# Expert stage of a one-core trunk kernel: gathered rows turned by VectorE instead of TensorE, low parts shared with GpSimd

## The chip, the cores and the metric

The kernel runs on one core of one Trainium2 chip, as one program. The metric is the device time of an execution in microseconds. Each of the core's engines (TensorE, VectorE, ScalarE, GpSimd and SyncE) runs its own instruction stream, and the streams meet only in semaphores.

## The reference, cut to what matters

The reference is one layer of a decoder trunk: three gated token mixers, an output projection, a layer norm, a mixture of experts with a router, and a second layer norm. The change touches the experts only. Each of 1024 tokens goes to two of 32 experts:

```python
def expert_block(args):
    xblk, e = args                                   # 128 gathered rows of 1024 features
    h = jax.nn.silu(xblk @ w_gate[e]) * (xblk @ w_up[e])   # 1024 x 512 each
    return h @ w_down[e]                             # 512 x 1024
y = jnp.zeros((N, D)).at[tok_sorted].add(yb[dest] * gate_sorted[:, None])
```

All of it is float32, and the kernel keeps that accuracy by splitting each operand in two.

## The kernel before

The stage `experts` handles one block of 128 slots for each of the 32 experts; an expert with more tokens than that is finished in a later stage. A product of two float32 matrices is computed as three products of a short type (`times`, lines 167 to 169): high by high, high by low, low by high. The high part is a cast (`fp32r`) by ScalarE, the low part is the full value minus the high part, by VectorE (`low_w`, L3515, for weights). An expert has three weight matrices of 2 MB: gate, up and down. Each lands in one of the buffers `landed0` to `landed2` in two halves of 1 MB, is cast into `high` (L3444) and subtracted into `low` (L3515), both half by half. When a half has been subtracted, SyncE issues the load of the same half for the next expert.

The tokens of an expert lie scattered in `x1_d` in device memory (the profile calls it `x_d`). GpSimd gathers 128 rows of 4 KB with one indirect DMA (`gather`, L3239) into `xb`, two buffers deep. As the matmul needs the features on the partitions, TensorE turns the block with eight transposes into PSUM (`turn_x`, L3357). ScalarE casts the result (L3438), and VectorE subtracts (`low_x`, L3509), reading PSUM.

The bodies are written out as follows, with e the expert:

- TensorE: gate(e), up(e), down(e-1), `turn_x`(e+2), `turn_h`(e). Gate, up and down are 24 matmuls of 512 columns each. `turn_h` (L3378) turns the hidden block in four transposes.
- ScalarE: silu(e), casts of gate(e+1) and up(e+1), copy of the result y(e-1) out of PSUM (L3459), casts of down(e), cast of x(e+2), cast of the hidden block (L3454).
- VectorE: low parts of gate(e+1), the product silu times up (`times_up`, L3523), low parts of up(e+1) and down(e), low part of x(e+2), low part of the hidden block (`low_h`, L3527).
- GpSimd: scatter of y rows (L3329) and the next gather. It does no arithmetic in this stage.

The order of each engine is fixed by this code. Every wait is on a counting semaphore; `low_ready`, `x_low_ready`, `x_turned`, `used` and `y_kept` are the ones that matter here.

Of the kernel before, what the change touches and what calls it, by code (L numbers as in the profile page):

```python
# [15 lines left out]
P = 128  # L16
# [3225 lines left out]

def part_half(t, h):
    return t[:, h * PART:(h + 1) * PART]
# [10 lines left out]
def experts(nc, k):  # L3255


    with Space(nc, "ex") as s:
# [15 lines left out]
        affinity, summed, shared, over_last = (s.sem(n) for n in ("affinity", "summed", "shared", "over_last"))  # L3274
        ended, block_expert, over_row = s.sb("ended", [P, 16, E]), s.sb("block_expert", [P, 16]), s.sb("over_row", [P, 16])
# [15 lines left out]
        with s.block() as block:  # L3291
            @block.sync
            def _(sp):
                def load(e, part):
                    for h in range(2):
                        sp.wait_ge(low_ready[part], 2 * e - 1 + h)
                        load_expert(sp, k, e, part, h)
# [11 lines left out]
                for n, to in enumerate(X1_LANDED):  # L3309
                    sp.wait_ge(low_ready[to], 2 * (E, E - 1)[n])  # L3310
                    if n == 0:
                        sp.wait_ge(k.landing[LAST_DOWN][1], 16 * E + 16)
                    sp.dma_start(k.landed[to][:, :].rearrange("p (t d) -> p t d", d=D), k.x1_d[n * HALF:(n + 1) * HALF, :].rearrange(
# [6 lines left out]
            def _(pool):  # L3320
# [18 lines left out]
                for e in range(E - 4, E):  # L3339
                    scatter(e)  # L3340

            @block.tensor
            def _(pe):
# [65 lines left out]
                pairs(pe, body, 0, E // 2 - 2, 1)  # L3409
                body(E - 3, 1)  # L3410
                body(E - 2, 0, False)
                gate_up(E - 1, 1)
                pe.wait_ge(low_ready[2], 2 * (E - 1))
                pe.wait_ge(h_low_ready, E)
# [15 lines left out]
            def _(act):  # L3430
# [3 lines left out]
                def high_x(e, b):  # L3434
# [3 lines left out]
                    nc.scalar.copy(xt[b][0][:, :, :], ps_x[:, :, :]).then_inc(x_high_ready, 1)  # L3438
# [39 lines left out]
                def body(e, b, more=True):  # L3478
# [594 lines left out]
```

## Time and profile before

| | |
|---|---|
| median of 3 runs | 2149.32 us (2149.32 to 2153.16) |
| the profiled execution | 2151.73 us |
| its span, first to last instruction | 2149.9 us |
| busy share of the span: TensorE, VectorE, ScalarE, GpSimd | 96%, 59%, 43%, 24% |
| mean granted TensorE clock | 0.987 of full speed |

The span is what the trace covers; 1.8 us of the profiled time lie around it. The busy shares are means over stages with different limits. The expert stage covers about the last quarter of the span (from 1517 us), and there the picture is a different one from the mean.

### The profile page before, as it was taken

To read this page: it belongs to the slowest core of one execution; us is meant where nothing else is said; L and a number is where in the kernel's file an instruction comes from. 1 tells how busy PE (TensorE), PEld (TensorE's weight loads), DVE (VectorE), ACT (ScalarE), POOL (GpSimd) and SP (SyncE) were. 2 spreads that over 40 slices of the span, in tenths; PEclk is the share of its full clock that TensorE was granted. 3 is DMA by queue.
4 is the path that set the end of the run, shared out by engine and by line. 5 is a ranking of instruction groups with operands and counts; after the bars stand their busy time and mean duration, and the time that the engine had idled before them with its cause. 6 is when DMAs were issued, how large, how long until landed. Compare 5 with 4: busy or idle time off the path is not lost. (4 is left out here: it accounts for less than half of the span.)

```text
span 2149.9 us, 36515 instructions
## 1 busy us (share of the span) xinstructions
PE 2064.1 (96%) x14738; PEld 1673.4 (78%) x14739; DVE 1271.1 (59%) x1286; ACT 925.1 (43%) x1067; POOL 505.4 (24%) x357
## 2 busy tenths in 40 slices
PE   8999899999999999999999999998899999999996
PEld 6777677767787887888887788787688888888882
DVE  4767422234410565356478723455798888888885
ACT  4662122242101553022246421001577777777763
POOL 4232311112340002233323332200122222222200
PEclk9999999999999999999999999999899999999998
DMA  4445534424431554321143522321699999999986
GB/s 151 138 122 191 180 114 128 128 97 152 158 133 42 128 114 147 119 67 41 49 133 118 175 85 98 118 100 59 250 406 390 386 387 386 383 381 388 382 335 240
DMA packets 138137, 408.48 MB, mean 190 GB/s; under 512 B 38736, under 2 KB 60112, under 8 KB 112800
## 3 DMA queue, kind: packets, MB, share of 16 engines
q1 hardware_dynamic: 123104, 367.40, 48.3%
q10 hardware_dynamic: 5552, 22.02, 2.7%
q0 software_dynamic: 9360, 17.32, 2.1%
q8 instruction: 91, 1.49, 0.3%
q14 instruction: 30, 0.25, 0.0%
HBM read 353.53 MB, written 69.93 MB: 197 GB/s over the span
## 5 line engine op out<-in xcount | busy, mean ns | idle before, releaser
L3515 DVE TENSOR_TENSOR ex_sb_low<-landed,high 128x2048 fp32r<-128x2048 f32 x192 | 431.2, 2287 | 61.2 <-ACT high L3444 57.7
L3444 ACT CAST high<-landed 128x2048 fp32r<-128x2048 f32 x186 | 346.4, 1912 | 38.6 <-PE ex_ps_u L169 37.3
L3329 POOL DMA_INDIRECT y_rows<-ex_sb_y,slot_row x32 | 32.2, 1006 | 438.9 <-ACT ex_sb_y L3459 420.8
L167 PE MATMUL ex_ps_g<-high,ex_sb_xt 128*128 128x512 f32 x260 | 104.6, 402 | 2.4 <-DVE ex_sb_xt L3509 2.4
L169 PE MATMUL ex_ps_g<-high,ex_sb_xt 128*128 128x512 f32 x260 | 102.3, 393 | 0.0
L168 PE MATMUL ex_ps_g<-ex_sb_low,ex_sb_xt 128*128 128x512 f32 x260 | 102.1, 393 | 0.0
L167 PE MATMUL ex_ps_u<-high,ex_sb_xt 128*128 128x512 f32 x260 | 101.3, 390 | 0.5 <-DVE ex_sb_low L3515 0.5
L168 PE MATMUL ex_ps_u<-ex_sb_low,ex_sb_xt 128*128 128x512 f32 x260 | 101.2, 389 | 0.0
L169 PE MATMUL ex_ps_u<-high,ex_sb_xt 128*128 128x512 f32 x260 | 101.2, 389 | 0.0
L169 PE MATMUL ex_ps_y<-high,ex_sb_ht 128*128 128x512 f32 x248 | 96.7, 390 | 0.0
L167 PE MATMUL ex_ps_y<-high,ex_sb_ht 128*128 128x512 f32 x248 | 96.6, 389 | 0.0
L168 PE MATMUL ex_ps_y<-ex_sb_low,ex_sb_ht 128*128 128x512 f32 x248 | 96.5, 389 | 0.0
L3239 POOL DMA_INDIRECT xb<-x_d,slot_token x32 | 84.7, 2646 | 35.9 <-PE ex_ps_x L3357 17.5
L167 PE MATMUL rc_ps_g<-x_high,next_high 128*128 128x512 f32 x144 | 60.9, 423 | 3.7 <-PEq L353 2.1
L167 PE MATMUL ri_ps_a<-x_high,next_high 128*128 128x512 f32 x128 | 52.0, 406 | 8.3 <-DVE x_low L778 8.3
L167 PEld LDWEIGHTS ex_ps_g<-high,ex_sb_xt 128*128 128x128 f32 x260 | 49.7, 191 | 12.3 <-DVE ex_sb_xt L3509 2.6
L167 PE MATMUL mg_ps_g<-x_high,next_high 128*128 128x512 f32 x144 | 56.2, 390 | 2.4 <-ACTq L2579 1.8
L167 PEld LDWEIGHTS ex_ps_u<-high,ex_sb_xt 128*128 128x128 f32 x260 | 48.8, 188 | 10.9 <-issue 0.9
L169 PEld LDWEIGHTS ex_ps_g<-high,ex_sb_xt 128*128 128x128 f32 x260 | 49.2, 189 | 10.4
L168 PE MATMUL rc_ps_g<-x_low,next_high 128*128 128x512 f32 x144 | 57.3, 398 | 0.0
L1597 ACT ACTIVATE fp_sb_qk_high<-fp_ps_t 128x1024 fp32r<-128x1024 f32 x8 | 8.2, 1028 | 114.0 <-PE fp_ps_t L169 114.0
L169 PE MATMUL rc_ps_g<-x_high,next_low 128*128 128x512 f32 x144 | 56.8, 395 | 0.0
(665 smaller groups left out, 5549.9 us busy)
## 6 DMA issues: line engine op xcount, KB each, us to landing
landed<-exp_up SPq DMA_DIRECT2D x64, 1024.0 KB, 8.2
landed<-exp_gate SPq DMA_DIRECT2D x64, 1024.0 KB, 7.6
landed<-exp_down SPq DMA_DIRECT2D x62, 1024.0 KB, 8.3
chunk_ch<-slab SPq DMA_DIRECT2D x4, 2048.0 KB, 7.5
merged_d<-room SPq DMA_DIRECT2D x16, 512.0 KB, 3.0
landed<-ssm_c SPq DMA_DIRECT2D x16, 512.0 KB, 4.9
cb_sb_y<-y_rows SPq DMA_DIRECT2D x16, 512.0 KB, 9.7
si_sb_w<-w_tiles SPq DMA_DIRECT2D x14, 512.0 KB, 3.6
```

The source lines that it names most:

```text
L167: nc.tensor.matmul(out, lhs[0], rhs[0], start=start, stop=False)
L168: nc.tensor.matmul(out, lhs[0], rhs[1], start=False, stop=False)
L169: return nc.tensor.matmul(out, lhs[1], rhs[0], start=False, stop=stop)
L1597: nc.scalar.activation(qk_high[n % 2][:, :], ps[n % 2][:, :, :].rearrange("p a b -> p (a b)"), ACT.Copy, scale=HD ** -0.5 if n < pairs els ...
L3239: pool.indirect_dma_start(k.xb[b][:, :], None, k.x1_d, bass.IndirectOffsetOnAxis(ap=k.slot_token[:, e:e + 1], axis=0), bounds_check=T - 1, ...
L3329: pool.indirect_dma_start(k.y_rows, bass.IndirectOffsetOnAxis(ap=k.slot_row[:, e:e + 1], axis=0), y[e % 2][:, :], None, bounds_check=2 * T ...
L3444: nc.scalar.copy(part_half(high[part], h), part_half(k.landed[part], h)).then_inc(high_ready[part], 1)
L3515: nc.vector.tensor_tensor(part_half(low[part], half), part_half(k.landed[part], half), part_half(high[part], half), ALU.subtract).then_inc ...
```

## The change

1. The turn. For experts 3 to 31 VectorE turns the rows, with one `transpose` instruction that turns each 32 by 32 block by itself. For this to give the features on the partitions, the rows have to be laid out beforehand: partition 32q+i gets quarter q of the row of slot 32g+i, for each of four groups g. So the gather is cut in four indirect DMAs of 128 pieces of 1 KB, whose indices (4 times the token number plus q) are made once, at the start of the stage, by 16 small matmuls on TensorE and one VectorE instruction. The turned block lies in SBUF (`x_full`, one buffer) and not in PSUM.
2. The low part of x. GpSimd subtracts it (`low_x`), between the second and the third quarter gather, as it can read SBUF and not PSUM. VectorE's `low_x` is left for experts 0 to 2.
3. The last quarter of the down weights' low part (1024 of 4096 columns) goes from VectorE to GpSimd (`low_last_w`). TensorE waits for it before the last of the four row blocks, and the load of the second half of the next down weights waits for it too.
4. Order. VectorE turns x(e+2) at the end of body e, behind `low_h`. ScalarE casts x(e+1) between the gate and the up weights instead of x(e+2) behind the down weights, and copies y(e-1) out at the end of the body.

```diff
@@ GpSimd
+                def low_last_w(e):
+                    pool.wait_ge(high_ready[2], 2 * e + 2)
+                    nc.gpsimd.tensor_tensor(low[2][:, LAST_AT:], k.landed[2][:, LAST_AT:], high[2][:, LAST_AT:], ALU.subtract
+                                            ).then_inc(low_last, 1)
+
+                def low_x(e):
+                    pool.wait_ge(x_low_ready, e + 1)
+                    pool.wait_ge(x_high_ready, e + 1)
+                    nc.gpsimd.tensor_tensor(xt[e % 2][1][:, :, :], x_full[:, :, :], xt[e % 2][0][:, :, :], ALU.subtract
+                                            ).then_inc(x_low_ready, 1)
...
-                for e in range(2, E):
-                    pool.wait_ge(x_turned, e + 1)
-                    gather(pool, k, e, e % 2)
+                for e in range(2, E + 2):
+                    if e < E:
+                        pool.wait_ge(x_turned, e + 1)
+                    if e == FIRST_QUARTERED:
+                        pool.wait_ge(quarters_ready, 1)
+                    if e < FIRST_QUARTERED:
+                        gather(pool, k, e, e % 2)
+                    elif e < E:
+                        gather_quarters(pool, k, quarter, e, e % 2, 0)
+                    if e - 2 >= FIRST_QUARTERED:
+                        low_x(e - 2)
+                    if FIRST_QUARTERED <= e < E:
+                        gather_quarters(pool, k, quarter, e, e % 2, 1)
+                    if e >= 3:
+                        low_last_w(e - 3)
                     if e >= 4:
                         scatter(e - 4)
@@ TensorE
+                            if half == 0 and c == FF - 1:
+                                pe.wait_ge(low_last, e + 1)
...
-                def body(e, b, more=True):
+                def body(e, b):
                     gate_up(e, b)
                     down(e - 1, 1 - b)
-                    if more:
-                        turn_x(e + 2, b)
                     turn_h(e, b)
@@ ScalarE
                     silu(e)
                     high_w(e + 1, 1 - b, 0)
+                    if with_x:
+                        high_x(e + 1, 1 - b)
                     high_w(e + 1, 1 - b, 1)
+                    high_w(e, b, 2)
+                    high_h(e)
                     keep_y(e - 1, 1 - b)
-                    high_w(e, b, 2)
-                    if more:
-                        high_x(e + 2, b)
-                    high_h(e)
@@ VectorE
+                def turn_x(e, b):
+                    dve.wait_ge(x_in[b], 32 * e - 32 + 16 * b)
+                    dve.wait_ge(x_low_ready, e + 1)
+                    nc.vector.transpose(x_full[:, :, :].rearrange("p k (g t) -> p g k t", g=PER_HEAD),
+                                        xb[b][:, :].rearrange("p (g t k) -> p g k t", g=PER_HEAD, k=KD)).then_inc(x_turned, 1)
...
                     low_w(e, b, 2)
+                    low_h(e)
                     if more:
-                        low_x(e + 2, b)
-                    low_h(e)
+                        turn_x(e + 2, b)
```

GpSimd's program in the body of an expert, before; L3329 is the scatter of a result, L3239 the gather of whole rows:

```order
L3329 DMA y_rows<-ex_sb_y,slot_row 2048x1024
L3239 DMA xb<-x_d,slot_token 128x1024
```

and now; L3254 is a quarter gather, L3368 the low part of x, L3362 the last quarter of the down weights' low part, L3356 the scatter:

```order
L3254 DMA xb<-x_d,ex_sb_quarter 128x256 x2
L3368 TENSOR_TENSOR ex_sb_xt<-ex_sb_x_full,ex_sb_xt 128x1024
L3254 DMA xb<-x_d,ex_sb_quarter 128x256 x2
L3362 TENSOR_TENSOR ex_sb_low<-landed,high 128x1024
L3356 DMA y_rows<-ex_sb_y,slot_row 2048x1024
```

Two instructions have become seven, and the subtraction of x stands behind two gathers.

VectorE's body before, in its second half of the loop; L3515 are low parts of weights, L3523 the product with silu, L3509 the low part of x, L3527 that of the hidden block:

```order
L3523 TENSOR_TENSOR ex_sb_h<-ex_sb_gate,ex_ps_u 128x512
L3515 TENSOR_TENSOR ex_sb_low<-landed,high 128x2048 x4
L3508 REGISTER_ALU
L3509 TENSOR_TENSOR ex_sb_xt<-ex_ps_x,ex_sb_xt 128x1024
L3527 TENSOR_TENSOR ex_sb_ht<-ex_ps_h,ex_sb_ht 128x512
```

and now; L3581, L3589 and L3593 are the same three kinds, L3574 is the turn:

```order
L3589 TENSOR_TENSOR ex_sb_h<-ex_sb_gate,ex_ps_u 128x512
L3581 TENSOR_TENSOR ex_sb_low<-landed,high 128x2048 x3
L3581 TENSOR_TENSOR ex_sb_low<-landed,high 128x1024
L3593 TENSOR_TENSOR ex_sb_ht<-ex_ps_h,ex_sb_ht 128x512
L3572 ISA
L3573 REGISTER_ALU
L3574 STREAM_TRANSPOSE ex_sb_x_full<-xb 128x4x8x32
```

The fourth weight subtraction behind the product is half as wide, the subtraction of x is gone, and the turn closes the body.

## Rows read from the trace of the kernel before

**Rows 1.** Busy time by window, two stretches of the expert stage.
```profile
core 0: us, PE busy (x) PEld busy (x) DVE busy (x) ACT busy (x) POOL busy (x), PEclk, DMA share, GB/s
1560.00:1600.00 40.00, 40.00 (x192) 33.63 (x191) 35.16 (x21) 32.67 (x24) 10.81 (x6) 1.00 1.01 411
1800.00:1840.00 40.00, 40.00 (x189) 33.55 (x189) 35.99 (x22) 31.32 (x23) 7.81 (x4) 1.00 1.00 389
```

**Rows 2.** Waits, 1600 to 2080 us: who waited for whom, total, times, longest.
```profile
DVE ex_sb_low L3515 <- ACT high L3444: 54.2, 42, 1.8
ACT ex_sb_y L3459 <- PE ex_ps_y L169: 47.3, 27, 1.8
ACT high L3444 <- PE ex_ps_u L169: 32.2, 27, 1.2
```

**Rows 3.** Timeline, TensorE at a body's end: start, duration, instruction.
```profile
1807.32 1.04 PE L3357 MATMUL ex_ps_x<-mats,xb 128*128 128x128 f32 x8
...
1808.20 0.65 PE L3378 MATMUL ex_ps_h<-mats,ex_sb_h 128*128 128x128 f32 x4
...
1808.61 0.48 PE L167 MATMUL ex_ps_g<-high,ex_sb_xt 128*128 128x512 f32 x1
```

**Rows 4.** Timeline of GpSimd: two scatters, twelve bodies apart.
```profile
1596.69 1.01 POOL L3329 DMA_INDIRECT y_rows<-ex_sb_y,slot_row  x1 [13.59 <-ACT ex_sb_y L3459]
...
1809.41 1.01 POOL L3329 DMA_INDIRECT y_rows<-ex_sb_y,slot_row  x1 [13.59 <-ACT ex_sb_y L3459]
```

**Rows 5.** Timeline, ScalarE and VectorE from a silu on.
```profile
1814.36 0.60 ACT L3449 ACTIVATE ex_sb_gate<-ex_ps_g 128x512 f32<-128x512 f32 x1 [0.74 <-PE ex_ps_g L169]
...
1814.85 3.71 ACT L3444 CAST high<-landed 128x2048 fp32r<-128x2048 f32 x2
...
1816.79 4.49 DVE L3515 TENSOR_TENSOR ex_sb_low<-landed,high 128x2048 fp32r<-128x2048 f32 x2
1821.20 0.68 DVE L3523 TENSOR_TENSOR ex_sb_h<-ex_sb_gate,ex_ps_u 128x512 f32<-128x512 f32 x1
1821.80 4.49 DVE L3515 TENSOR_TENSOR ex_sb_low<-landed,high 128x2048 fp32r<-128x2048 f32 x2
```

**Rows 6.** Timeline, GpSimd's gathers and what VectorE did beside them.
```profile
1517.04 1.07 POOL L3239 DMA_INDIRECT xb<-x_d,slot_token  x1 [9.83 <-DVE slot_token L3183]
1517.92 4.49 DVE L3515 TENSOR_TENSOR ex_sb_low<-landed,high 128x2048 fp32r<-128x2048 f32 x2 [1.75 <-ACTq L3462]
1518.42 2.66 POOL L3239 DMA_INDIRECT xb<-x_d,slot_token  x1 [0.30 <-issue]
...
1523.58 0.99 POOL L3239 DMA_INDIRECT xb<-x_d,slot_token  x1 [2.50 <-PE ex_ps_x L3357]
1523.86 1.23 DVE L3509 TENSOR_TENSOR ex_sb_xt<-ex_ps_x,ex_sb_xt 128x1024 fp32r<-128x1024 f32 x1 [1.44 <-ACT ex_sb_xt L3438]
```

**Rows 7.** Timeline of an earlier stage, subtractions of GpSimd and VectorE side by side.
```profile
1289.39 1.29 DVE L2783 TENSOR_TENSOR x_low<-ssm,x_high 128x512 fp32r<-128x512 f32 x2
1291.15 5.11 DVE L2783 TENSOR_TENSOR x_low<-ssm,x_high 128x512 fp32r<-128x512 f32 x4 [0.47 <-ACT x_high L2757]
1291.87 2.63 POOL L194 TENSOR_TENSOR mg_sb_w_low<-mg_sb_w,mg_sb_w_high 128x1024 fp32r<-128x1024 f32 x1 [0.18 <-POOL mg_sb_w_high L192]
...
1302.72 1.22 DVE L2797 TENSOR_TENSOR room<-room,ssm_zs 128x1024 f32<-128x1024 f32 x1
1302.74 3.45 POOL L194 TENSOR_TENSOR next_low<-mg_sb_w,next_high 128x1024 fp32r<-128x1024 f32 x1 [0.18 <-POOL next_high L192]
```

**Rows 8.** GpSimd's subtraction with VectorE quiet: minimum, median, maximum in ns.
```profile
L194 POOL TENSOR_TENSOR fp_sb_w_low<-fp_sb_w,fp_sb_w_high x4: 2388/2395/2397, 553.8 to 621.5; 128x1024 fp32r<-128x1024 f32 x4
```

**Rows 9.** Groups of VectorE, 1024 elements of one input or scanned.
```profile
L803 DVE TENSOR_SCALAR ri_sb_kk<-ri_sb_kx,cols 128x1024 f32<-128x1024 f32 x4 | 3.6, 908 | 0.1
...
L3509 DVE TENSOR_TENSOR ex_sb_xt<-ex_ps_x,ex_sb_xt 128x1024 fp32r<-128x1024 f32 x32 | 39.0, 1218 | 6.5 <-ACT ex_sb_xt L3438 6.5
...
L795 DVE TENSOR_TENSOR_SCAN landed<-rwkv_mats,landed 128x1024 f32<-128x1024 f32 x4 | 9.1, 2283 | 6.1 <-ACT landed L675 6.1
```

**Rows 10.** DMA queues, 1800 to 1900 us: packets, MB, share of 16 engines.
```profile
q1 hardware_dynamic: 4904, 35.73, 92.4%
q0 software_dynamic: 1548, 2.67, 7.0%
```

**Rows 11.** Small matmuls of an earlier stage, 128 of them.
```profile
L2992 PE MATMUL op_ps_l<-op_sb_w_r,op_sb_xt 128*128 128x32 f32 x128 | 15.2, 275 | 1.1 <-ACT op_sb_xt L3036 1.1
```

More of the change, by code:

```diff
@@ L3240, in gather, with gather_quarters @@
                             bounds_check=T - 1, oob_is_err=False).then_inc(k.x_in[b], 16)
+FIRST_QUARTERED = 3
+LAST_AT = (FF - 1) * D
+def gather_quarters(pool, k, quarter, e, b, half):
+    rows = k.x1_d.rearrange("t (q d) -> (t q) d", q=PER_HEAD)
+    for g in (2 * half, 2 * half + 1):
+        at = slice(g * D // PER_HEAD, (g + 1) * D // PER_HEAD)
+        pool.indirect_dma_start(k.xb[b][:, at], None, rows,
+                                bass.IndirectOffsetOnAxis(ap=quarter[:, g * E + e:g * E + e + 1], axis=0),
+                                bounds_check=PER_HEAD * T - 1, oob_is_err=False).then_inc(k.x_in[b], 16)
 def part_half(t, h):
@@ L3295, in load @@
                     for h in range(2):
+                        if part == 2 and h == 1:
+                            sp.wait_ge(low_last, e)
                         sp.wait_ge(low_ready[part], 2 * e - 1 + h)
@@ L3400, in _ @@
                 turn_h(0, 0)
-                def body(e, b, more=True):
+                pe.wait_ge(tokens_kept, 1)
+                for g in range(PER_HEAD):
+                    for q in range(PER_HEAD):
+                        m = nc.tensor.matmul(ps_quarter[q * BLK:(q + 1) * BLK, g * E:(g + 1) * E],
+                                             mat(k, "ident", BLK, g * BLK), token_f[:, :], start=True, stop=True,
+                                             skip_group_check=True)
+                m.then_inc(quarters_turned, 1)
+                def body(e, b):
                     gate_up(e, b)
                     down(e - 1, 1 - b)
-                    if more:
-                        turn_x(e + 2, b)
                     turn_h(e, b)
-                pairs(pe, body, 0, E // 2 - 2, 1)
-                body(E - 3, 1)
-                body(E - 2, 0, False)
+                pairs(pe, body, 0, E // 2 - 1, 1)
                 gate_up(E - 1, 1)
                 pe.wait_ge(low_ready[2], 2 * (E - 1))
+                pe.wait_ge(low_last, E - 1)
                 pe.wait_ge(h_low_ready, E)
@@ L3437, in high_x @@
                         act.wait_ge(used[1], e)
-                    nc.scalar.copy(xt[b][0][:, :, :], ps_x[:, :, :]).then_inc(x_high_ready, 1)
+                    src = ps_x if isinstance(e, int) and e < FIRST_QUARTERED else x_full
+                    nc.scalar.copy(xt[b][0][:, :, :], src[:, :, :]).then_inc(x_high_ready, 1)
                 def high_w(e, b, part):
@@ L3514, in low_w @@
                         dve.wait_ge(high_ready[part], 2 * e + 1 + half)
-                        nc.vector.tensor_tensor(part_half(low[part], half), part_half(k.landed[part], half),
-                                                part_half(high[part], half), ALU.subtract).then_inc(low_ready[part], 1)
+                        at = slice(half * PART, LAST_AT if part == 2 and half == 1 else (half + 1) * PART)
+                        nc.vector.tensor_tensor(low[part][:, at], k.landed[part][:, at], high[part][:, at], ALU.subtract
+                                                ).then_inc(low_ready[part], 1)
                 def times_up(e):
@@ L3539, in _ @@
                 low_h(0)
+                dve.wait_ge(quarters_set, PER_HEAD)
+                dve.wait_ge(quarters_turned, 1)
+                nc.vector.tensor_scalar(quarter[:, :], ps_quarter[:, :], float(PER_HEAD), quarter_of[:, :], ALU.mult, ALU.add
+                                        ).then_inc(quarters_ready, 1)
                 def body(e, b, more=True):
```

22 lines of the change are left out of this document (17 added, 5 removed).

## The prediction

> **What bounds the kernel now.** I read the page's slices first, then the windows, the waits, and last the timelines of the expert stage. In two windows of 40 us TensorE is busy for 40.00, at full clock; VectorE is busy for 36, ScalarE for 31 to 33, GpSimd for 8 to 11, and the DMA engines for all of it [rows 1]. From busy shares alone three things could bind: TensorE, VectorE or DMA. The waits decide. Between 1600 and 2080 us VectorE waits for ScalarE, and ScalarE for TensorE's matmuls; TensorE has no row, and a landing has none [rows 2]. So the stage is TensorE's. Twelve bodies take 1809.41 - 1596.69 = 212.72 us, 17.73 us each [rows 4].
>
> What VectorE has to spare is little. Per body it does six subtractions of 2.2 us, one of 1.22 and two of 0.68, some 16 of 17.73 us.
>
> **The change, part by part.** The sum goes by the length of a body, as the bodies repeat.
>
> *The turn leaves TensorE.* From the first of the eight transposes to the first of `turn_h` it is 1808.20 - 1807.32 = 0.88 us [rows 3]. It goes from 29 bodies (turns of experts 3 to 31). TensorE alone would need 17.73 - 0.88 = 16.85 us a body, and 29 x 0.88 = 25.5 us is the most that this edit can give.
>
> *What is late next.* Gate(e+1) now waits for GpSimd's subtraction of x(e+1). What does that cost? GpSimd's subtraction of 1024 elements takes 2.39 us with VectorE quiet [rows 8]. It does not run beside VectorE's subtractions from SBUF. At 1302.72 VectorE begins one of 1.22 us and GpSimd, 0.02 later, needs 3.45 instead of 2.39: it stood for about the 1.2 and then ran. The other way round, four VectorE subtractions that take 4 x 0.645 = 2.58 us (two took 1.29) took 5.11 with one GpSimd subtraction among them, 2.53 more [rows 7]. So each shuts the other out for its whole length, and the one that waits gets its turn at the next end. A VectorE instruction that reads PSUM does not do this: beside one a gather takes 0.99 us, but 2.66 us beside subtractions from SBUF; those began at 1517.92 and the first ended near 1520.17, so that the gather ended, at 1521.08, about 0.9 behind that end [rows 6]. VectorE's pair took its usual 4.49 there, so a gather waits and costs VectorE nothing.
>
> The Trainium skill bears on this. Its page "Advanced Engine Details and Errata", section "VectorE Performance Modes", says that GpSimd and two-port VectorE instructions block each other, and its table gives `tensor_tensor` no two-port mode; by that table alone the subtractions would run side by side and the body would last 16.85 us. The trace does not agree with such a reading (3.45 and 5.11 us above). The page "GPSIMD Engine Reference", "Key points", counts instructions with two SBUF inputs among those that contend, which is what the rows show.
>
> *The chain of a body.* From gate(e) to silu 1814.36 - 1808.61 = 5.75 us [rows 3, 5]. From there, by [rows 5]: 0.49 to the first cast of the next gate weights; 1.94 to their first subtraction; 4.41 for the two of them, to the product; 0.60 to the first subtraction of the up weights. Meanwhile GpSimd has two quarter gathers ahead of `low_x`. Both are asked for while VectorE subtracts gate weights. The first ends about 0.9 us behind the end of the first of these, the second 0.9 us behind the end of the second. VectorE's product, which leaves the way free, lasts 0.60 us; GpSimd asks 0.3 us too late and waits for the first subtraction of the up weights, 2.25 us (half of 4.49). Then its own 2.39, and about 0.10 to TensorE's start. Sum: 5.75 + 0.49 + 1.94 + 4.41 + 0.60 + 2.25 + 2.39 + 0.10 = 17.93 us. That is 0.20 above 17.73. GpSimd's subtractions stand in the 28 bodies of experts 3 to 30: 28 x 0.20 = 5.6 us slower. With each GpSimd subtraction at 2.63 as in [rows 7], it is 18.17 and 12 us.
>
> *VectorE's own load.* Five subtractions at 2.205 (4.41 / 2) are 11.03, the short one half of 2.29, 1.14, together 12.17 us with both inputs in SBUF; the product and `low_h` 0.60 each; the turn. No row shows a turn. The nearest are one pass over 1024 elements: 0.91 us for one input from SBUF, 1.22 for two with PSUM, and 2.28 for a scan [rows 9]. I take 1.22, as it is written once per element at VectorE's usual pace, and keep 0.91 and 2.28 for the range. VectorE then has 15.6 us, less than 16, but GpSimd shuts it out for up to 2 x 2.39 = 4.78 more. Below: all of that falls beside the product, `low_h`, the turn and waits; the two engines' sum of SBUF time is 12.17 + 4.78 = 16.95 us, the floor of the body. Above: none of it does, 15.6 + 4.78 = 20.4 us, or 19.2 if at least the product and `low_h`, which read PSUM, cover 1.2 of it. Break-even at 17.73 needs 2.6 of the 4.78 us to be covered. The chain above has 2.4 of them covered by `low_h` and the turn behind the short subtraction, and 0 to 0.2 by waits for ScalarE, which is why it comes out near break-even.
>
> The page "Vector Engine (DVE) Microarchitecture Reference", section "The reshape front-end and per-opcode configuration", states that a transpose sustains one element per cycle per lane. At VectorE's 0.96 GHz (the skill's figure) that is 1.07 us and a fixed part, an estimate from that page; no run here shows it yet, and the sum would stay as it is.
>
> *Quarter gathers.* Four DMAs of 128 pieces in place of one. For GpSimd: at least 4 x 0.99, at most 4 x 2.66 us [rows 6]; with 0.3 between them, the two subtractions and the scatter, 4 x 1.3 + 4.78 + 1.3 = 11.3 us at least, 18 at most. The last two gathers and `low_last_w` have no reader within 6 us, so this costs nothing as long as GpSimd's body stays under 17.9. For the DMA engines: the software queue has 7.0% of their time, half of it the gathers [rows 10]. If pieces of 1 KB cost as much as rows of 4 KB, it grows by 3 x 3.5% = 10.5%, which is the bound above; if bytes decide, nothing. I take nothing: 411 GB/s were moved in 1560 to 1600 against 389 [rows 1], so there is some room.
>
> *Moved work.* ScalarE copies y(e-1) later by two casts of weights and one of the hidden block, some 4 us, and down(e) reads that PSUM only a gate and an up later, 11 us; hidden. The cast of x stands between gate and up casts, beside TensorE's up; 1.0 us of ScalarE's slack of 1.2 [rows 2] ahead of the up casts, hidden. *Setup:* 16 small matmuls at 15.2 / 128 = 0.12 us [rows 11] and a wait for the copied tokens, 2 us once.
>
> *Sum.* 2151.7 + 5.6 + 2 = 2159.3 for the profiled execution. The median lies 2.4 below it: 2157.
>
> **The rivals.**
> *A, TensorE binds again.* If the second gather ends before the product does (0.3 us is all that it lacks), GpSimd's 2.39 us begins beside the product, and the subtraction of x is 2.25 earlier. The body falls to the SBUF floor, 16.95 us: 29 x 0.78 = 22.6 less, 2 for the setup: 2129. For it: the margin of 0.3 us is thin, and quarter gathers may be quicker than full ones. Against: VectorE then starts its up subtractions 1.8 us late, and what is won in one place stands as a shut-out in another.
> *B, slower, one mechanism:* the turn itself takes the shared way to SBUF. Then GpSimd's last subtraction is not covered by it, VectorE loses another 1.2 us in each body, and more if the turn is slow: 19.2 us, 28 x 1.47 = 41 more, 2192. It decides as soon as `low_last_w` and the turn follow each other in time. For it: the turn reads and writes SBUF. Against: it has one input.
> *C, DMA binds.* The DMA engines are 0.99 to 1.00 busy at 17.73 us. If that is real work, no body is shorter than 17.5, and with dearer pieces it is 17.6 to 18.1: 2146 to 2162. Against: nobody waits for a landing [rows 2], and 411 GB/s would give 17.73 x 389 / 411 = 16.8 us.
>
> **How the numbers follow.** Chances: the forecast with its own range of 17.65 to 18.3 us, 0.38; A 0.28; B 0.22; C 0.10; something else 0.02. No change is within 0.2%, 4.3 us or 0.15 us a body, about what can be told. Faster: A and half of C, 0.33. Same: an eighth of all from the forecast's low side and some of C, 0.16. Slower: the rest, 0.51. The likeliest one's own range is 2148 to 2170. The wide one reaches from A's floor to B: 2126 to 2194.
>
> **What would show it.** Right: TensorE idle before its first gate matmul, ended by GpSimd's subtraction, 0.5 to 1.5 us a body; GpSimd's subtractions at 2.4 to 4.6 us, VectorE's stretched; scatters 17.9 us apart. A: TensorE without idle time and scatters 17.0 apart. B: the turn stretched when GpSimd subtracts, VectorE busy throughout, scatters 19 apart. C: waits on landings. I am wrong on the hinge if GpSimd's subtraction of x begins before the up weights' one does.

## The result and the profile after

The changed kernel takes 2277.73 us (median of 4 runs, 2266.98 to 2291.56); the kernel before, on the same chip, 2149.32 us (4 runs, 2149.18 to 2153.16). The ratio is 1.0596, with a 95% interval of 1.0573 to 1.0619: 6% slower. The forecast was 2157.0 and the range 2126 to 2194. Slower was right, the size was not: 128 us where 8 were forecast.

The profiled execution took 2291.56 us, its span is 2289.8. First the windows of the same kind as [rows 1] (busy time of each engine in 40 us, then granted clock, DMA share and rate):

```profile
core 0: us, PE busy (x) PEld busy (x) DVE busy (x) ACT busy (x) POOL busy (x), PEclk, DMA share, GB/s
1560.00:1600.00 40.00, 28.45 (x109) 23.12 (x110) 23.79 (x14) 19.20 (x14) 30.00 (x13) 0.77 0.85 334
1800.00:1840.00 40.00, 28.42 (x115) 22.89 (x114) 37.32 (x21) 24.69 (x18) 33.41 (x12) 0.84 0.96 346
1900.00:1940.00 40.00, 37.72 (x169) 30.89 (x167) 40.00 (x20) 30.41 (x23) 32.74 (x14) 1.00 0.94 339
```

TensorE is no longer busy throughout, and the three windows differ. The first is the start of the expert stage. The second holds a long gap of TensorE, and the granted clock has fallen with it: 0.84 is a mean of the two levels of 2.4 and 1.2 GHz. In the third VectorE is busy for 40.00 of 40. So three things are to be explained: the start, the gap and the full VectorE. DMA is none of them: the queues moved less than before, and from 1620 to 2200 us no engine waits for a landing.

The waits from 1620 to 2200 us (total, times, longest), against [rows 2]:

```profile
ACT ex_sb_gate L3508 <- PE ex_ps_g L169: 161.4, 27, 13.8
PE ex_ps_g L167 <- POOL ex_sb_xt L3368: 106.6, 16, 9.8
```

TensorE now has a row: its gate matmuls wait for GpSimd's subtraction of x, 16 times and 6.7 us each. That is the wait that the prediction named, but it foresaw 0.5 to 1.5 us of it in a body. From the list of groups (busy us, mean ns, idle before):

```profile
L3581 DVE TENSOR_TENSOR ex_sb_low<-landed,high 128x2048 fp32r<-128x2048 f32 x192 | 471.3, 2507 | 106.6 <-ACT high L3503 104.8
L3254 POOL DMA_INDIRECT xb<-x_d,ex_sb_quarter x116 | 290.7, 2506 | 94.6 <-DVE ex_sb_x_full L3574 41.2
L3574 DVE STREAM_TRANSPOSE ex_sb_x_full<-xb 128x1024 f32<-128x1024 f32 x29 | 61.4, 2118 | 29.5 <-POOL ex_sb_xt L3368 29.5
```

The turn takes 2.12 us; 1.22 was taken. VectorE's weight subtractions have grown from 431.2 to 471.3 us in all, although one in six of them is now half as long.

**The regular body.** VectorE's product `times_up` is a good mark, since VectorE makes it once a body and in order. From the fourth product to the last there are 28 bodies. Five take 20.2 to 20.3 us, against 17.73 [rows 4]; ten take 25.8 to 27.3, and eleven, each just behind such a long one, 19.2 to 19.3; the last two take 21.4 and 15.2. The 20.2 is called the regular body here, because all bodies have it when no gather is held (the run with pauses, below). One of them, VectorE and then GpSimd (start, duration):

```profile
1914.72 4.45 DVE L3581 TENSOR_TENSOR ex_sb_low<-landed,high 128x2048 fp32r<-128x2048 f32 x2
1919.09 0.68 DVE L3589 TENSOR_TENSOR ex_sb_h<-ex_sb_gate,ex_ps_u 128x512 f32<-128x512 f32 x1
1919.68 12.67 DVE L3581 TENSOR_TENSOR ex_sb_low<-landed,high 128x2048 fp32r<-128x2048 f32 x4
1932.28 0.68 DVE L3593 TENSOR_TENSOR ex_sb_ht<-ex_ps_h,ex_sb_ht 128x512 fp32r<-128x512 f32 x1
1932.88 2.12 DVE L3574 STREAM_TRANSPOSE ex_sb_x_full<-xb 128x1024 f32<-128x1024 f32 x1
```

```profile
1915.58 2.29 POOL L3254 DMA_INDIRECT xb<-x_d,ex_sb_quarter  x1 [2.56 <-DVE ex_sb_x_full L3574]
1918.18 1.86 POOL L3254 DMA_INDIRECT xb<-x_d,ex_sb_quarter  x1 [0.31 <-issue]
1920.06 2.37 POOL L3368 TENSOR_TENSOR ex_sb_xt<-ex_sb_x_full,ex_sb_xt 128x1024 fp32r<-128x1024 f32 x1
1922.60 2.88 POOL L3254 DMA_INDIRECT xb<-x_d,ex_sb_quarter  x1 [0.16 <-issue]
1925.78 1.90 POOL L3254 DMA_INDIRECT xb<-x_d,ex_sb_quarter  x1 [0.30 <-issue]
1927.70 3.58 POOL L3362 TENSOR_TENSOR ex_sb_low<-landed,high 128x1024 fp32r<-128x1024 f32 x1
```

There is no gap on VectorE. Its four subtractions of up and down weights take 12.60 us from the first start to `low_h`; undisturbed they take 7.8. The difference of 4.8 is 2 x 2.4, the two subtractions of GpSimd that fall into them, each at its whole length. So 12.17 (weights) + 1.20 (product, `low_h`) + 2.05 (turn, start to start of the next) + 4.78 = 20.2 us. `low_last_w` ends at 1931.28, before `low_h` starts at 1932.28. It was to run beside `low_h` and the turn, and runs just ahead of them.

GpSimd's subtraction of x starts at 1920.06, 0.3 us behind the product's end at 1919.77, and runs at once. The up subtraction that VectorE began at 1919.68 does the waiting:

```profile
1919.68 4.91 DVE L3581 TENSOR_TENSOR ex_sb_low<-landed,high 128x2048 fp32r<-128x2048 f32 x1
```

In the bodies of 19.2 us GpSimd asks earlier, runs beside the product and delays that subtraction by 1.6 us only (3.9 in place of 2.3).

**The long body.** VectorE, GpSimd and TensorE in one (26 to 27 us from product to product instead of 20):

```profile
1823.62 4.45 DVE L3581 TENSOR_TENSOR ex_sb_low<-landed,high 128x2048 fp32r<-128x2048 f32 x2
1827.98 0.68 DVE L3589 TENSOR_TENSOR ex_sb_h<-ex_sb_gate,ex_ps_u 128x512 f32<-128x512 f32 x1
1828.58 7.82 DVE L3581 TENSOR_TENSOR ex_sb_low<-landed,high 128x2048 fp32r<-128x2048 f32 x4
...
1839.69 2.05 DVE L3574 STREAM_TRANSPOSE ex_sb_x_full<-xb 128x1024 f32<-128x1024 f32 x1 [2.68 <-POOL ex_sb_xt L3368]
1850.23 2.29 DVE L3581 TENSOR_TENSOR ex_sb_low<-landed,high 128x2048 fp32r<-128x2048 f32 x1 [8.49 <-ACT high L3503]
```

```profile
1824.48 4.48 POOL L3254 DMA_INDIRECT xb<-x_d,ex_sb_quarter  x1 [2.61 <-DVE ex_sb_x_full L3574]
1829.27 8.01 POOL L3254 DMA_INDIRECT xb<-x_d,ex_sb_quarter  x1 [0.31 <-issue]
1837.31 2.35 POOL L3368 TENSOR_TENSOR ex_sb_xt<-ex_sb_x_full,ex_sb_xt 128x1024 fp32r<-128x1024 f32 x1
1839.82 1.00 POOL L3254 DMA_INDIRECT xb<-x_d,ex_sb_quarter  x1 [0.16 <-issue]
```

```profile
1839.79 0.79 PE L167 MATMUL ex_ps_g<-high,ex_sb_xt 128*128 128x512 f32 x1 [8.63 <-POOL ex_sb_xt L3368]
```

Here the first gather was not let in at the end of the first gate subtraction, only at the end of the second (4.48 us instead of 2.29). The second gather then came at 1829.27, 0.6 us behind the end of the product at 1828.66, and was held through all four subtractions: 8.01 us, to 1837.28, 0.96 behind the end of the fourth at 1836.32. GpSimd's subtraction of x stands behind it, TensorE waits 8.63 us for that, and ScalarE and VectorE for TensorE (8.49).

That wait holds a second cost, which is TensorE's own. It had stood idle for 8.63 us, and from 1838 to 1844 us its granted clock is 0.50, the level of 1.2 GHz. From the first gate matmul to silu it takes 1847.81 - 1839.79 = 8.02 us, where 5.75 were enough before:

```profile
1847.81 0.60 ACT L3508 ACTIVATE ex_sb_gate<-ex_ps_g 128x512 f32<-128x512 f32 x1 [11.98 <-PE ex_ps_g L169]
```

In the ten long bodies this stretch takes 7.2 to 8.7 us, some 21 us in all above 5.8.

Eleven of the 116 gathers take 8.0 us; the shortest of the others take 1.0.

Beside the turn a gather takes 1.00 us, as beside nothing (1839.82). So the turn does not take the shared way (the way to SBUF on which the two engines' subtractions shut each other out).

**The start.**

```profile
1570.65 5.63 DVE L3581 TENSOR_TENSOR ex_sb_low<-landed,high 128x2048 fp32r<-128x2048 f32 x2 [10.57 <-ACT high L3503]
```

```profile
1558.81 3.46 POOL L3362 TENSOR_TENSOR ex_sb_low<-landed,high 128x1024 fp32r<-128x1024 f32 x1
```

```profile
1562.33 0.80 PE L167 MATMUL ex_ps_y<-high,ex_sb_ht 128*128 128x512 f32 x1 [6.73 <-POOL ex_sb_low L3362]
```

GpSimd makes the first `low_last_w` only behind the four gathers of expert 3, and these wait 27.4 us for the quarter indices, which TensorE and VectorE make first. TensorE's first down product waits 6.73 us for it, and VectorE idles 10.57.

**The account.** The marks are the fourth and the last product. Before:

```profile
1590.84 0.68 DVE L3523 TENSOR_TENSOR ex_sb_h<-ex_sb_gate,ex_ps_u 128x512 f32<-128x512 f32 x1
...
2084.85 0.69 DVE L3523 TENSOR_TENSOR ex_sb_h<-ex_sb_gate,ex_ps_u 128x512 f32<-128x512 f32 x1 [3.49 <-issue]
```

After:

```profile
1609.48 0.68 DVE L3589 TENSOR_TENSOR ex_sb_h<-ex_sb_gate,ex_ps_u 128x512 f32<-128x512 f32 x1
...
2225.00 0.69 DVE L3589 TENSOR_TENSOR ex_sb_h<-ex_sb_gate,ex_ps_u 128x512 f32<-128x512 f32 x1 [3.98 <-issue]
```

The profiled executions differ by 2291.56 - 2151.73 = 139.8 us. By the fourth product 1609.48 - 1590.84 = 18.6 of it are there: the start, with the first long body in it. The 28 bodies behind it take 615.5 instead of 494.0 us, 121.5 more: 28 x (20.2 - 17.64) = 72 if all were regular, and 50 for the long ones among them, some 21 of it through the lower clock. The tail is unchanged.

### The profile page after: what moved, and what is told of

Its sections match the earlier page's. It is cut to its first block and busy times, and to the rows that moved or that the text cites. A ratio compares the mean times of both kernels' runs of the same rounds, so it can differ in the third digit from the quotient of the medians.

```text
span 2289.8 us, 36418 instructions
## 1 busy us (share of the span) xinstructions
PE 2077.9 (91%) x14538; PEld 1672.8 (73%) x14539; DVE 1339.6 (59%) x1288; ACT 925.3 (40%) x1067; POOL 920.0 (40%) x508
## 5 line engine op out<-in xcount | busy, mean ns | idle before, releaser
L3581 DVE TENSOR_TENSOR ex_sb_low<-landed,high 128x2048 fp32r<-128x2048 f32 x192 | 471.3, 2507 | 106.6 <-ACT high L3503 104.8
L3254 POOL DMA_INDIRECT xb<-x_d,ex_sb_quarter x116 | 290.7, 2506 | 94.6 <-DVE ex_sb_x_full L3574 41.2
L167 PE MATMUL ex_ps_g<-high,ex_sb_xt 128*128 128x512 f32 x260 | 119.4, 459 | 118.3 <-POOL ex_sb_xt L3368 115.8
L167 PEld LDWEIGHTS ex_ps_g<-high,ex_sb_xt 128*128 128x128 f32 x260 | 57.3, 221 | 134.1 <-issue 119.5
L169 PE MATMUL ex_ps_g<-high,ex_sb_xt 128*128 128x512 f32 x260 | 112.8, 434 | 0.0
L3368 POOL TENSOR_TENSOR ex_sb_xt<-ex_sb_x_full,ex_sb_xt 128x1024 fp32r<-128x1024 f32 x29 | 89.2, 3075 | 58.7 <-ACT ex_sb_xt L3497 58.3
L3362 POOL TENSOR_TENSOR ex_sb_low<-landed,high 128x1024 fp32r<-128x1024 f32 x31 | 94.7, 3055 | 16.6 <-ACT high L3503 16.1
L3508 ACT ACTIVATE ex_sb_gate<-ex_ps_g 128x512 f32<-128x512 f32 x32 | 19.2, 600 | 189.4 <-PE ex_ps_g L169 189.4
L3574 DVE STREAM_TRANSPOSE ex_sb_x_full<-xb 128x1024 f32<-128x1024 f32 x29 | 61.4, 2118 | 29.5 <-POOL ex_sb_xt L3368 29.5
L169 PEld LDWEIGHTS ex_ps_g<-high,ex_sb_xt 128*128 128x128 f32 x260 | 56.7, 218 | 13.8
L168 PEld LDWEIGHTS ex_ps_g<-ex_sb_low,ex_sb_xt 128*128 128x128 f32 x260 | 57.3, 220 | 11.8
L167 PEld LDWEIGHTS ex_ps_y<-high,ex_sb_ht 128*128 128x128 f32 x248 | 47.2, 190 | 17.0 <-POOL ex_sb_low L3362 7.2
```

Of the source, the lines that this page charges most:

```text
L167: nc.tensor.matmul(out, lhs[0], rhs[0], start=start, stop=False)
L168: nc.tensor.matmul(out, lhs[0], rhs[1], start=False, stop=False)
L169: return nc.tensor.matmul(out, lhs[1], rhs[0], start=False, stop=stop)
L3254: pool.indirect_dma_start(k.xb[b][:, at], None, rows, bass.IndirectOffsetOnAxis(ap=quarter[:, g * E + e:g * E + e + 1], axis=0), bounds_ch ...
L3362: nc.gpsimd.tensor_tensor(low[2][:, LAST_AT:], k.landed[2][:, LAST_AT:], high[2][:, LAST_AT:], ALU.subtract).then_inc(low_last, 1)
L3368: nc.gpsimd.tensor_tensor(xt[e % 2][1][:, :, :], x_full[:, :, :], xt[e % 2][0][:, :, :], ALU.subtract).then_inc(x_low_ready, 1)
```

## The experiments

The theory that they test: a body is as long as VectorE's work plus those parts of GpSimd's subtractions that nothing covers, with three terms: the shut-outs (4.8 us), the turn (2.05), and on top the gathers that are held too long. Twelve runs follow. "Body" is the time from one product of VectorE to the next; a mean body is taken from the fourth to the 31st. Runs of before beside them: 2151.68, 2151.05 and 2151.03 us for the three sets of four.

### Subtractions given back to VectorE

**The last quarter of the down weights back on VectorE** (GpSimd keeps x):

```diff
-                        at = slice(half * PART, LAST_AT if part == 2 and half == 1 else (half + 1) * PART)
+                        at = slice(half * PART, (half + 1) * PART)
```

> The last quarter of the down weights' low part goes back to VectorE; GpSimd keeps the subtraction of x and the quarter gathers. Theory S (each GpSimd subtraction shuts VectorE out for its whole 2.35 us, and VectorE is the bound): VectorE needs 6 x 2.205 + 1.2 (product and hidden block) + 2.07 (turn) + 2.35 = 18.85 us in a regular body, where the changed kernel has 20.2; 28 bodies at 1.1 over 17.73 make about 2181 us, and up to 2240 if the second quarter gather still starves for 8 us in every second body. Rival L (the turn's 2.1 us alone makes VectorE late): without shut-outs VectorE has 16.5 us, less than TensorE's 16.85: 2128 us.

Measured: 2262.59 us, ratio 1.0541 [1.0491, 1.0592]. The regular body is 19.1 us and seven gathers still take over 7 us, up to 9.1. The ledger says 20.2 - 2.39 (one shut-out less) + 1.14 (VectorE's own) = 18.95. The median falls by 15 us only and lies above the 2240 that was expected at most, since long bodies stay: six of the 28 take 27.1 to 28.5 us.

**x back on VectorE, from the turned copy** (GpSimd keeps the down quarter):

```diff
+                def low_x_full(e, b):
+                    dve.wait_ge(x_high_ready, e + 1)
+                    nc.vector.tensor_tensor(xt[b][1][:, :, :], x_full[:, :, :], xt[b][0][:, :, :], ALU.subtract
+                                            ).then_inc(x_low_ready, 1)
```

> VectorE subtracts x from SBUF itself, GpSimd keeps the last quarter of the down weights' low part. Theory S: 12.17 + 1.14 + 1.2 + 2.07 + 2.35 = 18.9 us a body, about 2183 us, and some 12 us more if the late start of the stage (TensorE's first down product waits for GpSimd behind four gathers) stays: 2183 to 2195. Rival G (it is the gathers ahead of the subtraction of x, starved by VectorE, that cost the time, and the shut-outs little): no reader waits on the gathers any more, 17.7 us a body or less, 2150 us or less.

Measured: 2192.22 us, 1.0210 [1.0160, 1.0259], too near 2% to call it clearly slower. Ten of the 28 bodies of the profiled execution are 18.7 to 18.9 us; by the ledger 20.2 - 2.39 + 1.14 = 18.95. That is the same regular body as in the first run within 0.4 us, but 70 us less in the median: now TensorE does not stand behind the gathers for x. Five gathers still take 8 us; their harm is down to some 3.5 us a body (22.2 against 18.7), through `low_last_w`. And 14 bodies are only 16.5 to 17.4 us: a held gather or scatter has moved GpSimd's queue so far that `low_last_w` falls beside `low_h` and the turn (one at 1923.20 takes 2.52 us). The profiled execution, 2174.32 us, is the fastest of four that reach 2202.63; how many bodies the slower ones have of each kind was not seen.

**Both on VectorE.** 

> VectorE makes both low parts; GpSimd only gathers and scatters. Theory S: nothing shuts VectorE out; 13.23 + 1.14 + 1.2 + 2.07 = 17.64 us a body, VectorE still the bound, and the late start is gone: 2147 us, no change. Rival D (quarter pieces of 1 KB slow the DMA engines, or the weights land late): stays above 2180 us with waits on landings. Rival L would have 2128 us or less for a turn of 1.2 us, which this is not.

Measured: 2150.31 us, 0.9998 [0.9983, 1.0012]. From the fourth product on all bodies are 17.6 us, with VectorE busy for 440.00 of 440 us; the ledger says 12.17 + 1.14 + 1.20 + 1.14 + 2.05 = 17.7. Seventeen gathers take over 7 us, up to 9.1, and no body is longer for it: a held gather costs only what stands behind it in GpSimd's queue. What is left of the change here, the turn on VectorE, is worth 0.1 us a body: 17.6 set by VectorE against 17.73 set by TensorE.

### The cover that the prediction assumed

**Down quarter on GpSimd, beside `low_h` and the turn.** To the kernel of the second run (x on VectorE) comes a wait that puts `low_last_w` behind VectorE's last weight subtraction, and ahead of the gathers:

```diff
                 def low_last_w(e):
                     pool.wait_ge(high_ready[2], 2 * e + 2)
+                    pool.wait_ge(low_ready[2], 2 * e + 2)
```

> As e2, but GpSimd's subtraction of the last quarter waits until VectorE has made all its own low parts of that expert, so that it runs beside the hidden block's low part (PSUM) and the turn, 2.7 us in which VectorE does not need the shared way; and it stands ahead of the gathers. Theory S: VectorE has 12.17 + 1.14 + 1.2 + 2.07 = 16.6 us, the shut-out of 2.35 us costs nothing, and TensorE is the bound again at 16.85 to 16.95 us: 28 x 0.8 = 22 less than before, 2127 to 2140 us with the late start. If a starved gather brings GpSimd late, the shut-out is back: 18.9 us, 2183 us. Rival L/G: no difference from e2.

Measured: 2148.34 us, 0.9984 [0.9973, 0.9995]. Regular body 16.8 us, TensorE without a break: by the ledger VectorE has 18.95 - 2.39 = 16.6, so TensorE's 16.85 binds, the floor of the prediction. So the covered body exists. The time misses the 2127 to 2140 expected: it is eaten by the start (one body there lasts 30.1 us) and two bodies of 22.8.

**Expert 3 still turned by TensorE and `low_last_w(0)` early.** `FIRST_QUARTERED` is 4.

> e4, and expert 3 is turned by TensorE as before, so that the quarter gathers begin with expert 4 and GpSimd subtracts expert 0's last quarter ahead of them. In e4 the first scatter came 27 us later than before the change, TensorE waiting for GpSimd behind four gathers. Theory: that is the price of the setup, and it goes: 2148 - 25 = 2123 us, with the two long bodies of e4 (25 us) still there. Rival (the late start is the chain turn, cast, subtraction of the first turned expert, which only moves one body on): 2140 to 2148 us.

Measured: 2142.69 us, 0.9959 [0.9943, 0.9976]. The fourth product is at 1591.8, 1 us behind before's: the start is repaired. In the run before it was at 1601.4, so that the repair gives 9.6 us and not the 25 expected, and the time lies in the rival's range. From there most bodies are 16.5 to 16.9 us, but the mean is 17.30. One regular stretch and one long:

```profile
1834.55 7.83 DVE L3589 TENSOR_TENSOR ex_sb_low<-landed,high 128x2048 fp32r<-128x2048 f32 x4
1842.29 0.69 DVE L3601 TENSOR_TENSOR ex_sb_ht<-ex_ps_h,ex_sb_ht 128x512 fp32r<-128x512 f32 x1
1842.89 2.21 DVE L3582 STREAM_TRANSPOSE ex_sb_x_full<-xb 128x1024 f32<-128x1024 f32 x1
```

```profile
1779.21 8.00 POOL L3254 DMA_INDIRECT xb<-x_d,ex_sb_quarter  x1 [0.31 <-issue]
...
1790.12 5.34 POOL L3356 DMA_INDIRECT y_rows<-ex_sb_y,slot_row  x1 [0.31 <-issue]
1795.49 2.35 POOL L3363 TENSOR_TENSOR ex_sb_low<-landed,high 128x1024 fp32r<-128x1024 f32 x1
...
1842.53 2.41 POOL L3363 TENSOR_TENSOR ex_sb_low<-landed,high 128x1024 fp32r<-128x1024 f32 x1 [2.59 <-DVE ex_sb_low L3589]
```

```profile
1797.89 0.79 PE L167 MATMUL ex_ps_y<-high,ex_sb_ht 128*128 128x512 f32 x1 [4.69 <-POOL ex_sb_low L3363]
```

At 1842.53 GpSimd's subtraction takes 2.41 us beside `low_h` and the turn, and the four subtractions ahead of them 7.83: neither lost anything. At 1779.21 a gather is held again, for 8.00 us, and the scatter behind it for 5.34, so `low_last_w` is late and TensorE waits 4.69.

**A short instruction between up and down.** The last kernel, with a memset of one column (0.06 us) ahead of the first down subtraction:

```diff
+                        if (part, half) in PAUSED:
+                            nc.vector.memset(pause[:, 6 * b + 2 * part + half:6 * b + 2 * part + half + 1], 0.0)
```

> e7 with one column written between VectorE's subtractions of the up and of the down weights, one 0.06 us instruction a body. Theory G: a starved gather then waits 4.4 us at most instead of 7, GpSimd is back in time for its subtraction, and e4's two long bodies (17 us together) go: 2106 to 2115 us. Rival (0.06 us is no way in): as e7.

Measured: 2140.34 us, 0.9955 [0.9938, 0.9971]. A miss: one gather of 8 us and seven between 4 and 7 remain, the mean body is 17.24. One such place is not enough.

**Four of them** (`PAUSED` names all subtractions that follow another without a wait). 

> The kernel of e7_covered_early with a one-column memset of 0.06 us ahead of four of VectorE's six weight subtractions of a body: those that follow another subtraction without a wait between. Theory (GpSimd gets in at any end that is followed by a short instruction): no gather above 5.7 us and no body above 18.5 us; VectorE, 39.7 of 40 us busy without the pauses, gets 0.24 us more a body and then sets it at about 17.0 us, against a mean of 17.34 in e7; 28 x 0.3 = 8 us less than e7: 2132 to 2136. Rival (what is left in e7 is the DMA queues, which moved 414 GB/s at best): the mean body stays at 17.2 to 17.3 with waits for landings, and the time at 2138 to 2142.

Measured: 2135.11 us, 0.9926 [0.9913, 0.9940], 5 runs from 2134.72 to 2135.52. Mean body 17.07, as the theory has it. One gather still takes 8.04 us, past three pauses, so the "no gather above 5.7" failed once in 112, and two bodies of 18.8 and 19.4 us break the "no body above 18.5". The DMA engines are 1.00 busy at 396 GB/s, and waits for landings of down weights appear (14.2 us in 440, 1.4 at the longest), which the kernel before had not: a part of what the rival named. This is the fastest kernel here, 0.7% below the kernel before, clear of the noise and under 2%.

### The held gathers

**The changed kernel with a pause ahead of each weight subtraction.** 

> The changed kernel with a write of one column (0.06 us, one operand) ahead of each of VectorE's subtractions of weights. Theory G with entry at any instruction that leaves the shared way free: no gather over 3 us, bodies of 20.2 + 0.4 = 20.6 us throughout, about 2240 us. Rival (GpSimd needs a longer stretch than 0.06 us to get in): gathers of 8 us as before and some 2290 us.

Measured: 2238.48 us, 1.0412 [1.0392, 1.0433]. All bodies of the run's middle are 20.2 to 20.3 us, and no gather takes over 2.89. No gather or scatter was passed over at any of the 85 ends with a pause behind them at which one waited. The long bodies alone are thus worth 2277.7 - 2238.5 = 39 us in the median and 55.8 in the profiled spans (2289.8 and 2234.0), where the account above had 50 and one more long body in the start. The run alone does not show that the pause is the way in, since it also moves every gather a little; two runs below have no held gather without any pause.

**GpSimd's subtraction of x ahead of all four gathers**, in place of between the second and the third:

```diff
-                    elif e < E:
-                        gather_quarters(pool, k, quarter, e, e % 2, 0)
                     if e - 2 >= FIRST_QUARTERED:
                         low_x(e - 2)
                     if FIRST_QUARTERED <= e < E:
+                        gather_quarters(pool, k, quarter, e, e % 2, 0)
                         gather_quarters(pool, k, quarter, e, e % 2, 1)
```

> GpSimd's order alone is changed: the subtraction of x stands ahead of all four quarter gathers. Theory G (the changed kernel's long bodies of 24.6 us come from the second quarter gather, which VectorE's uninterrupted subtractions hold up for 7 us while the subtraction of x, for which TensorE waits, stands behind it): the long bodies shorten to the regular 20.2 us, less 30 to 40 us, 2210 to 2245 us, TensorE's waits for the subtraction of x mostly gone. Rival S alone (only the shut-outs count): 2278 us as before, and the waits stay.

Measured: 2166.14 us, 1.0080 [1.0064, 1.0097]; expected was far more, and the miss taught most. From the fourth product on the bodies are 17.8 us, but for the last two. VectorE, then GpSimd:

```profile
1912.45 2.23 DVE L3573 STREAM_TRANSPOSE ex_sb_x_full<-xb 128x1024 f32<-128x1024 f32 x1
1914.62 5.18 DVE L3580 TENSOR_TENSOR ex_sb_low<-landed,high 128x2048 fp32r<-128x2048 f32 x2
1919.72 0.68 DVE L3588 TENSOR_TENSOR ex_sb_h<-ex_sb_gate,ex_ps_u 128x512 f32<-128x512 f32 x1
1920.32 9.42 DVE L3580 TENSOR_TENSOR ex_sb_low<-landed,high 128x2048 fp32r<-128x2048 f32 x4
```

```profile
1912.98 2.46 POOL L3362 TENSOR_TENSOR ex_sb_low<-landed,high 128x1024 fp32r<-128x1024 f32 x1
1915.61 2.89 POOL L3356 DMA_INDIRECT y_rows<-ex_sb_y,slot_row  x1 [0.17 <-issue]
1918.52 3.53 POOL L3368 TENSOR_TENSOR ex_sb_xt<-ex_sb_x_full,ex_sb_xt 128x1024 fp32r<-128x1024 f32 x1
1922.20 2.90 POOL L3254 DMA_INDIRECT xb<-x_d,ex_sb_quarter  x1 [0.15 <-issue]
```

`low_last_w` has come to stand at the turn (1912.98), which leaves the way free: 1.6 of its 2.4 us are covered, and the gate pair loses 0.73 (5.10 against 4.37). GpSimd's subtraction of x waits until the pair ends at 1919.72 and has the product's 0.6 us free, so that the four lose 1.5 (9.34 against 7.8). Together 2.3 us of shut-out instead of 4.8, and 20.2 - 2.5 = 17.7. Without a change of work the order on GpSimd alone is worth 112 us. In that are the held gathers too: here none takes over 2.92 us. Most of what is left to the kernel before is the start (the fourth product at 1599.5, 8.7 us late).

**One gather of whole rows in place of four of quarters.** 

> The changed kernel with the gather of a block as one instruction of whole rows in place of four of quarter rows. What is turned is then laid out otherwise, so the output is not the reference's. Theory (a long body comes of a gather that is held through four subtractions of VectorE, which can happen to the second of four): with one gather ahead of GpSimd's subtraction of x there is no such place, nearly all bodies are 20.2 us, and the time is 2230 to 2245. Rival (the four gathers' own time on GpSimd, about 8 us of 20, holds the subtractions back): bodies of 18 to 19 us, 2170 to 2200.

Measured: 2203.91 us, 1.0240 [1.0224, 1.0255]; bodies of 19.1 and 20.2 us, 19.57 in the mean, no gather over 4.48. No long body, as the theory had it, but 2203.91 lies below its 2230, and above the rival's 2200. With one gather ahead of it in place of two, GpSimd's subtraction of x runs beside the product in 17 of 25 bodies (it starts 1.2 us ahead of the product, waits for the end and takes 3.5 us), so a part of a shut-out went too. That the quarter gathers' own time on GpSimd decides the place of its subtractions is read from this and not tested by itself.

### The rest

**The kernel before with the down quarter on GpSimd.** 

> The kernel before with one part of the change alone: GpSimd makes the last quarter of the down weights' low part (between gather and scatter). TensorE is busy without a break in the kernel before (17.73 us a body) and VectorE has 4 of 40 us free. Theory (two subtractions shut each other out, but only a full VectorE pays for it): VectorE loses 1.14 us of work and gains up to 2.35 of shut-out, 1.2 of 1.8 free, so the time stays within 0.3% if GpSimd's subtraction is done before TensorE asks for it. Rival (a subtraction on GpSimd is a chain that TensorE waits for wherever it stands): 1 to 2 us a body, 2180 to 2210.

Measured: 2152.08 us, 1.0008 [0.9999, 1.0017], 10 runs; the body stays at 17.73. VectorE and GpSimd:

```profile
1917.29 5.63 DVE L3535 TENSOR_TENSOR ex_sb_low<-landed,high 128x2048 fp32r<-128x2048 f32 x2 [1.04 <-ACT high L3463]
```

```profile
1919.15 2.69 POOL L3343 TENSOR_TENSOR ex_sb_low<-landed,high 128x1024 fp32r<-128x1024 f32 x1 [11.84 <-ACT high L3463]
```

The shut-out is there (5.63 us for a full and a half-length subtraction that alone take 3.4), and nobody pays: VectorE still waits 1.04 us ahead of them, and TensorE is busy for 440.00 of 440.

**The turn reading in the order of the elements**, not every eighth:

```diff
-                                        xb[b][:, :].rearrange("p (g t k) -> p g k t", g=PER_HEAD, k=KD)).then_inc(x_turned, 1)
+                                        xb[b][:, :].rearrange("p (g k t) -> p g k t", g=PER_HEAD, k=KD)).then_inc(x_turned, 1)
```

> The changed kernel with VectorE's turn reading its elements in the order in which they lie, rather than every eighth. The output is then not the reference's. Theory (the step of 8 elements makes the turn slow): the turn takes 1.1 to 1.3 us, and the regular body 20.2 - 0.9 = 19.3. Rival (the turn takes 2.1 us for 1024 columns however they lie): nothing changes.

```profile
L3574 DVE STREAM_TRANSPOSE ex_sb_x_full<-xb 128x1024 f32<-128x1024 f32 x29 | 35.6, 1229 | 0.0
```

The turn takes 1.23 us instead of 2.12: the 0.89 are the step of eight. Every body is 19.3 us (20.2 - 0.9), and in this one execution of 2207.75 us no gather was held beyond 2.89. With the shorter turn the gathers fall otherwise against VectorE's ends; that this is why none was held is argued, from one execution.

## Why the prediction was wrong

- **TensorE's 0.88 us, the floor of 16.85.** Right: the covered kernels run at 16.8 to 16.9.
- **The chain of a body, 17.93 us.** Failed, twice over. Its term of 2.25 us, GpSimd waiting for the first up subtraction, was nothing in the regular body. The second gather ended 0.3 us behind the product, just as the chain had it, but GpSimd's subtraction of x ran at once, in 2.37 us, and the up subtraction, begun at 1919.68, took 4.91 instead of 2.28. (By the rows it begins first, so the sign set for the hinge does not tell this.) And the body is not 16.95 then, because VectorE and not the chain ends last.
- **VectorE's own load.** The step that decides. I took the "above" end for a bound and the chain for the value; the truth is the "above" end, 4.78 us with nothing covered. The assumption that failed, and that decides the 20.2 us, is "2.4 of them covered by `low_h` and the turn behind the short subtraction": `low_last_w` got its turn one subtraction earlier. It ended 1.0 us before `low_h` began. The regular bodies of the three runs that gave one or both subtractions back agree with the ledger to 0.3 us. With 2.5 us to be covered for break-even (20.2 - 17.73), I should have asked in which gap each of the two would have to start, and what would hold it back until then; nothing did.
- **A slip in the sum.** 12.17 + 1.20 + 1.22 is 14.6, not the 15.6 of the text, and "above" is then 19.4, not 20.4. The run with the quick turn measured 19.3. That 20.4 came near the measured 20.2 is luck, two errors that cancel: the slip of 1.0 and a turn 0.83 longer. With the right sum and the turn at 1.22, break-even needed 1.65 us of cover, not 2.6.
- **The turn at 1.22 us.** 2.12, inside the bounds of 0.91 and 2.28, and mis-sized by the step of 8 elements that it reads with. The Trainium skill's page "Vector Engine (DVE) Microarchitecture Reference", section "The reshape front-end and per-opcode configuration", gives one element per cycle and lane; at 0.96 GHz that is 1.07 us and a fixed part, an estimate. The run in the order of the elements agrees with it (1.23 us), the kernel's own turn does not (2.12 us).
- **"The one that waits gets its turn at the next end."** True at some ends only. Where VectorE's next subtraction follows without a wait, a gather may be passed over, at one end or at several running: 4.48, 8.01, 9.1 us. This put 39 us on the median and 56 on the profiled span, some 21 of it in the gate matmuls at the lower clock, and no rival held it. Both margins I worked with (2.66 us for a gather, 0.3 us missed at the product) were taken from single rows.
- **Setup 2 us.** 18.6 by the fourth product, of which a held gather is a part: 13.7 in the run with pauses, where none is held. I priced the 16 matmuls and did not follow `low_last_w(0)` through GpSimd's queue, behind four gathers that wait for those matmuls.
- **The rivals.** A: what it needed, the subtraction of x at once behind the product, came, though the gather was as late as the forecast had it, and it did not suffice. Its 16.95 us was reached in no run with both subtractions on GpSimd; 17.8 is the nearest. B: its sign, VectorE busy throughout, came true without its mechanism; the turn does not take the shared way (a gather of 1.00 us beside it, `low_last_w` of 2.41). C: not in this kernel, and a body of 17.07 us was reached below its 17.5; there waits for landings began to show.
- **The count of costs.** Of the 128 us in the median some 40 are held gathers, 72 the regular body (28 x 2.56: 0.83 the slow turn, and the rest the shut-outs less what VectorE had free), and the rest the start.

## What to carry to other kernels

When two engines shut each other out, add the whole of the one's time to the other's, and take off only what you can place: name the instruction that leaves the way free, and what makes the work start beside it. If nothing in the program makes it wait for that place, it need not be there. With x on VectorE, one semaphore wait and an earlier place in the queue took the regular body from 18.7 to 16.8 us; with both subtractions on GpSimd, another order alone took it from 20.2 to 17.8. And what stands behind a gather in a queue inherits its worst case, not its mean.

## What the runs showed of the hardware

- A GpSimd instruction that wants the way that VectorE's subtractions take can be passed over at several of their ends: a gather 8.0 us through four subtractions without a wait between them, a GpSimd subtraction 6.9 us (the second run, at 1905.96). Between 0 and 17 of 116 gathers in a run took over 7 us.
- Counted over the traces of all runs, a waiting gather or scatter was let in at 803 of 1040 ends behind which another subtraction followed at once, at 194 of 199 with a one-column memset behind them, and at all 333 with something else or a wait behind them. Two of the runs without any memset, x first and the turn in order, let in at every end. What decides at an end was not found.
- TensorE's granted clock was 0.50 (1.2 GHz) behind the idle stretches of 8.6 to 9.8 us, and the 24 gate matmuls behind them took up to 8.7 us to silu instead of 5.8.
- The changed kernel's four runs spread over 24.6 us, those of the last covered kernel over 0.8. That the number of held gathers differs from run to run would explain it, but only one execution of each kernel was traced.
- A VectorE transpose of 128 x 1024 elements took 1.23 us read in order and 2.12 read with a step of 8; beside the second a gather of 1.00 us and a GpSimd subtraction of 2.41 us lost nothing.
- A DMA share near 1.00 was not a ceiling: from 1620 to 2060 us the queues moved 385 GB/s at a share of 0.99 in the kernel before, and 396 at 1.00 in the fastest one.
